# Moving the factor products and gates of a feed-forward layer from second-level into first-level Strassen steps, and another order of the sums at its entry

## What is computed

```python
def layer_tail(x, attn, rw, attn_out_g, w_out, norm_ffn_g, w_gate, w_up, w_down):
    mix = jnp.concatenate([rmsnorm(attn, attn_out_g), rw], axis=-1)
    h = x + mix @ w_out
    u = rmsnorm(h, norm_ffn_g)                      # 1056 x 1024
    return h + (jax.nn.silu(u @ w_gate) * (u @ w_up)) @ w_down     # 2816 hidden columns
```

## Time and profile before

| | |
|---|---|
| median of three runs | 1822.84 us (1821.5 to 1827.82) |
| the profiled execution | 1822.36 us |
| its span, first to last instruction | 1820.6 us |
| mean granted clock of TensorE | 0.983 |
| busy: TensorE, its weight loads | 1724.9 us (95%), 1300.2 us (71%) |
| busy: VectorE, ScalarE, GpSimd | 1046.7 us (57%), 444.9 us (24%), 738.1 us (41%) |
| tail from the end of the out product | from about 950.8 us to the end |
| steps 1 to 51 | 977.4 to 1534.6 us |

### The profile page before, as it was taken

The page is one execution under the profiler, slowest core; times in us unless marked ns, Lnnn a source line. Parts: engine busy times, 40 slices in busy tenths (PEclk is TensorE's granted clock), DMA queues, the critical chain, the costliest instruction groups (busy, mean ns, idle before and its releaser), DMA issues.

```text
span 1820.6 us, 34845 instructions
## 1 busy us (share of the span) xinstructions
PE 1724.9 (95%) x14612; PEld 1300.2 (71%) x14612; DVE 1046.7 (57%) x1703; ACT 444.9 (24%) x987; POOL 738.1 (41%) x551
## 2 busy tenths in 40 slices
PE   6999999999998998999998899999999999999999
PEld 4566666666665656666667777787777887788887
DVE  3767767767767675665257646554554545625422
ACT  3333333334334334665021111111111201000000
POOL 3563664565455440001333434343433431634332
PEclk9999999999999998999998999999999999999999
DMA  9443343334333326110512111111110112333421
GB/s 361 165 140 108 88 134 128 100 102 141 88 119 106 109 65 165 47 47 1 216 50 103 35 35 46 35 47 41 41 38 33 47 35 76 119 95 113 143 92 64
DMA packets 95921, 169.36 MB, mean 93 GB/s; under 512 B 30395, under 2 KB 64011, under 8 KB 91542
## 3 DMA queue, kind: packets, MB, share of 16 engines
q1 hardware_dynamic: 87302, 119.29, 20.8%
q10 hardware_dynamic: 8464, 47.85, 7.5%
HBM read 136.40 MB, written 23.04 MB: 88 GB/s over the span
## 4 chain that ended last, share of the span: by engine, by line
PE 41%; DVE 9%; issue 1%; ACT 0%; DVEq 0%
PE psum L2811 37%; PE psum L2764 4%; DVE hid L3325 2%; DVE hid L3277 1%; DVE hid L3291 1%; DVE hid L3279 1%; DVE hid L3392 0%; DVE mixT L3393 0%; DVE u2c L3339 0%; DVE u2c L3350 0%; DVE u2c L3336 0%; DVE u_sum L3398 0%; PE psum L2799 0%; DVE u2c L3334 0%; DVE u2c L3357 0%
## 5 line engine op out<-in xcount | busy, mean ns | idle before, releaser
L2811 PE MATMUL psum<-mixT,wA 128*128 128x264 f32 x996 | 237.7, 390 | 0.0
L2811 PEld LDWEIGHTS psum<-mixT,wA 128*128 128x128 f32 x996 | 192.2, 193 | 34.0
L535 PE MATMUL psum<-wsl,xt 128*128 128x368 f32 (+2 forms) x716 | 190.2, 441 | 2.8 <-ACT proj L1182 1.7
L2811 PE MATMUL psum<-hid,wA 128*128 128x264 f32 x614 | 150.1, 398 | 26.3 <-DVE u2c L3336 25.7
L2811 PEld LDWEIGHTS psum<-hid,wA 128*128 128x128 f32 x614 | 118.1, 194 | 50.5 <-DVE u2c L3336 29.5
L535 PEld LDWEIGHTS psum<-wsl,xt 128*128 128x128 f32 (+1 forms) x716 | 100.0, 169 | 61.5 <-issue 11.3
L2811 PE MATMUL psum<-u_sum,wA 128*128 128x264 f32 x532 | 130.2, 389 | 5.1 <-ACT con L3000 3.2
L3090 POOL TENSOR_TENSOR wA<-wA 128x512 f32<-128x512 f32 x22 | 29.1, 1324 | 231.4 <-DMA wA<-in_w_up 122.5
L2811 PEld LDWEIGHTS psum<-u_sum,wA 128*128 128x128 f32 x532 | 101.1, 191 | 25.0 <-ACT con L3000 4.4
L2811 PE MATMUL psum<-slot,wA 128*128 128x264 f32 x480 | 111.8, 386 | 3.2 <-DVE slot L3409 3.2
L2811 PEld LDWEIGHTS psum<-slot,wA 128*128 128x128 f32 x480 | 91.1, 190 | 19.1 <-DVE u_sum L3398 3.6
(11 more groups left out here) (427 smaller groups left out, 3514.5 us busy)
## 6 DMA issues: line engine op xcount, KB each, us to landing
wsl<-in_w_in ACTq DMA_DIRECT2D x18, 1472.0 KB, 6.2
wA<-in_w_down SPq DMA_DIRECT2D x30, 704.0 KB, 4.3
slot<-in_w_in ACTq DMA_DIRECT2D x9, 1472.0 KB, 6.8
wA<-in_w_gate SPq DMA_DIRECT2D x44, 256.0 KB, 3.0
wA<-in_w_up SPq DMA_DIRECT2D x44, 256.0 KB, 2.9
mixed<-proj SPq DMA_DIRECT2D x8, 784.0 KB
xt<-in_x_tiles SPq DMA_DIRECT2D x9, 512.0 KB, 6.0
hid<-in_x_cols SPq DMA_DIRECT2D x8, 528.0 KB, 7.1
```

What stands on the lines that cost most here:

```text
L535: return pe.matmul(out, lhsT, rhs, start=start, stop=stop)
L2811: ins = pe.matmul(pb[bank][:, 0:NW], left(k), right(k), start=first and k == 0, stop=k == depth - 1, skip_group_check=not first)
```

## The change

For each quadrant of each unit a new function `home` names one first-level step and a slot in it: `EARLY_` (behind the sum `c11`, ahead of `c12`), `OWN` (between `c12` and `c21`) or `LATE_` (at the end). A quadrant that is complete after a first- or second-level step goes to the next first-level step. Quadrant 11 of a unit that isn't folded stays in its own step. Exceptions stand in `home`: double 0 goes to steps 6 and 8, the two quadrants 12 of double 7 stay at the end of their second-level step 39, and what is complete last (double 10) is done in step 51. `tasks(i, slot)` gives the gate quadrants, of which at most three go to the early slot and the rest to `OWN`, and the up quadrants. VectorE's new `gates` makes factor product j + 1 before gate product j; ScalarE makes `tanh` in the same order, in first-level steps ahead of `p5c` and `u2c`.

```diff
+        if q == 12 and not gate_unit(d, b) and not cut_in_two(d, 3):
+            return done, OWN
+        if q == 11 and not folded:
+            return at_step[1, F, 0] if d == 0 else done, EARLY_
+        if d == N_D - 1 and (folded or b):
+            return N_STEPS - 1, LATE_ if folded else EARLY_
+        if q == 12 and d == LATE_END - 1:
+            return done, LATE_
+        if d == 0:
+            first = not folded and b == 0 or q == 11
+            return (at_step[1, F, 0], EARLY_) if first else (at_step[1, F, 1], EARLY_)
+        if d == 1 and b == 0 and q in (11, 21):
+            return at_step[2, F, 0], EARLY_
+        i = done + 1
+        while STEPS[i][1] != F:
+            i += 1
+        return i, EARLY_
...
+        def gates(found):
+
+            for j, x in enumerate(found):
+                scale(x)
+                if j:
+                    gate(found[j - 1])
+            if found:
+                gate(found[-1])
...
         def first_level(i, d, b):
...
-            scales(early_scaled.get(i, []))
-            gates(i)
+            opened, found = tasks(i, EARLY_)
+            head = [x for x in found if x[0] == 22]
+            ups(head)
+            gates(opened)
+            ups([x for x in found if x not in head])
+            if i == at_step[0, F, 1]:
+                token_sums_of(2, 0, 4)
+                token_sums_of(3, 0, 4)
+            if i == at_step[N_D - 1, F, 1]:
+                down_sums_begun()
             if i == 0:
-                row_means()
+                row_factors()
...
             named(tt(two(place(12, d, b)), bank_pair(W), two(u2c), ALU.add), "c12_ok", n)
-            scales(own_third(i))
-            if i == 0:
-                row_factors()
+            opened, found = tasks(i, OWN)
+            ups(found)
+            gates(opened)
```

```diff
+        def down_sums_begun():
+
+            dve.wait_ge(s["hid_ok"], n_hid(at_step[N_D - 1, F, 0]))
+            c1 = slice(HT, HT + NW)
+            B12, B22 = hid[:, 0:FH - 1, c1], hid[:, FH:2 * FH - 1, c1]
+            named(tt(B12, B22, B12, ALU.subtract), "f3_ok", 1)
...
             if i == 0:
+                row_sums()
                 pe.wait_ge(s["t3_ok"], 1)
-                row_sums()
             pe.wait_ge(s["s3_ok"], u + 1)
             for nh in range(2):
                 pe.wait_ge(s["u2_ok"], 2 * n - 1 + nh)
                 product(X + nh, left(S3), half(B12u, nh), KH, "p7_ps", first=False)
-                if i == 0 and nh == 0:
-                    row_factors()
+            if i == 0:
+                row_factors()
```

More of the change, by code:

```diff
@@ L2586, in bank, with home @@
         return pb[i][:, 0:NW]
-    scaled_in, gated_in = {}, {}
+    EARLY_, OWN, LATE_ = 0, 1, 2
+    homes = {}
+    def home(x):
+        q, d, b = x
+        k = INNER.get(q, 0)
+        folded = k and after(d, b, k)
+        done = at_step[d, S, k] if folded else at_step[d, F, b]
+        if q == 12 and not gate_unit(d, b) and not cut_in_two(d, 3):
[15 more added lines that the diff above has]
+        return i, EARLY_
@@ L2605, in tail @@
-    own_third = lambda i: [x for x in scaled_in.get(i, []) if x == (12, STEPS[i][0], STEPS[i][2]) and STEPS[i][1] == F]
-    late_scaled = {i: [x for x in found if INNER.get(x[0], 0) and after(x[1], x[2], INNER[x[0]])] for i, found in scaled_in.items()}
-    early_scaled = {i: [x for x in found if x not in late_scaled[i] + own_third(i)] for i, found in scaled_in.items()}
+            for q in (22, 21, 11, 12):
+                homes.setdefault(home((q, d, b)), []).append((q, d, b))
+    is_gate = lambda x: gate_unit(*x[1:])
@@ L2609, in gate_of, with tasks @@
+    def tasks(i, slot):
+        early, own = homes.get((i, EARLY_), []), homes.get((i, OWN), [])
+        opened = [x for x in early if is_gate(x)]
+        ups = [x for x in early if not is_gate(x)]
+        if slot == EARLY_:
+            return opened[:3], sorted(ups, key=lambda x: x[0] != 22)
+        if slot == OWN:
+            return opened[3:], own
+        late = homes.get((i, LATE_), [])
+        return [x for x in late if is_gate(x)], [x for x in late if not is_gate(x)]
     def gate_of(x):
@@ L2993, in _ @@
             weighted(k, slice(0, TOK), "u_lo")
+        squares(KD - 2)
         act.wait_ge(s["ps_done"], 2 * KD)
@@ L2997, in _ @@
             weighted(k, slice(HT, TOK), "u_hi1")
+        squares(KD - 1)
         for k in (4, 5):
@@ L3021, in first_level @@
                 copy(two(place(11, d, b)), bank_pair(X)).then_inc(s["p1_ok"], 1)
-            if i == 0:
-                for last in (KD - 2, KD - 1):
-                    squares(last)
-            for x in early_scaled.get(i, []):
-                if gate_unit(*x[1:]):
-                    tanh(x)
+            for x in tasks(i, EARLY_)[0]:
+                tanh(x)
             all_read(i - 1)
+            if any(x[0] == 22 for x in tasks(i, EARLY_)[1]):
+                act.wait_ge(s["hid_ok"], n_hid(i - 1) + 1)
             act.wait_ge(s["p5_ps"], n)
@@ L3046, in second_level @@
             copy(first_in, bank(X)).then_inc(s["m1_ok"], 1)
-            for x in late_scaled.get(i - 1, []):
-                if gate_unit(*x[1:]):
-                    tanh(x)
             if not folds(d, k, 1):
@@ L3065, in _ @@
                 second_level(i, d, n)
-        for x in late_scaled.get(N_STEPS - 1, []):
-            if gate_unit(*x[1:]):
-                tanh(x)
         for n in range(len(DOWN)):
@@ L3360, in second_level @@
                 named(tt(o12, W, v2, ALU.add), "v12_ok", n)
-            last = late_scaled.get(i, [])
-            if i < N_STEPS - 1:
-                scales(last)
-                gates(i)
-            else:
-                scales([x for x in last if gate_unit(*x[1:])])
-                gates(i)
-                scales([x for x in last if not gate_unit(*x[1:])])
+            opened, found = tasks(i, LATE_)
+            gates(opened)
+            ups(found)
         for i, (d, what, n) in enumerate(STEPS):
```

91 lines of the change are left out of this document (34 added, 57 removed).

## The result

The changed kernel takes 1764.07 us as a median (1763.07 to 1764.33) against 1822.99 us (1821.5 to 1827.82): a ratio of 0.967, with a 95% interval of 0.965 to 0.969. That is 58.9 us, where 53 were forecast. The profiled execution took 1763.07 us, its span is 1761.3 us, and the mean granted clock rose from 0.983 to 0.992.

A forecast was written before the change was run, and what follows sets the result against it. TensorE, busy 95%, was taken as the bound, with time won only where it waits, mostly for VectorE, or runs at low clock. Entry 7.0 + steps 43 + down product 3.0 = 53 us off, 1769.8 as median, range 1762 to 1788.

The forecast's parts named there:

- The steps: Steps 1 to 51: waits and half clock, together 45.7 us, go, less 1 and 1.5 for new waits: 43 us gained.
- the wait of step 8: First-level step 8, which also has an up product and two more gates: a new cost of 1 us.
- the other one: Behind step 39, which keeps two up products at its end: u2c late for the next step, 1.5 us.
- t: Time of one VectorE multiplication in first-level steps, taken as 0.8 us; no wait up to 1.06 us in the L3299 steps.
- the formula: First-level steps: 4.5 + 4t + 1.94 = 10.7 in L3299 steps, 6.6 + 2t = 10.7 in steps starting with p11's copy.
- Rival 1: First-level steps: multiplications take 1.66 us there too, u2c comes 2.4 us late in five steps, 20 us, 1790; chance 0.12.
- rival 4: Eleven first-level steps with gates: three tanh delay p5c and u2c; slower from t = 2.9 us, about 1832; chance 0.03.
- The entry: Entry before step 1: earlier squares and sums let row sums start without a wait; 8.0 less 1.0 for clock, 7.0 us.
- rival 2: Entry: row sums and transposes let the clock fall to half, 4 to 5 us more, 1774; chance 0.15.
- The down product: First group of the down product: waits of 0.7 and 3.2 us go, 3.9, less 0.9 half clock: 3.0 us gained.

The follow-up runs named there:

- ups_after_v3: Changed kernel with the two up products at the end of step 39 made in step 40 behind its sums v22 and v21: 1764.41 us.
- best: Changed kernel with step 39's up products in step 40, GpSimd's first wide down-product sum held back, product five started on ten blocks: 1755.62 us.
- gates_plus1: Changed kernel with one more VectorE multiplication, which changes nothing, ahead of each of the 44 factor products: 1765.93 us.
- four_early: Changed kernel with up to four instead of three gates in the early slot, ahead of ScalarE's p5c and u2c: 1765.1 us.
- gates_plus3: Changed kernel with three more VectorE multiplications, which change nothing, ahead of each factor product: 1842.67 us, ratio 1.011 to the kernel before.
- entry_back: Changed kernel with the old order at the entry (squares, their sums, row sums, row factors, row means, token sums): 1772.88 us.
- f3_whole: Changed kernel with the first operand sum of the down product (f3) whole again, behind the last hidden result: 1764.7 us.
- before_again: The kernel before the change, unchanged, profiled a second time: 1821.17 us, down product 287.80 us.
- lone_steps: Changed kernel with six factor and six gate products of doubles 2, 4 and 6 put back into second-level steps between first-level ones: 1765.63 us.
- e3_later: Changed kernel with GpSimd's first 1408-wide sum of the down product held until VectorE has made the last up product: 1760.89 us.
- f3_whole_again: Second profile of the changed kernel with the operand sum f3 whole again: 1764.89 us, down product 287.80 us.

## Why the prediction was right

**The sign, the mechanism and the range were right; the sum was 6 us short.** 53 forecast, 58.9 measured, 1764.07 within 1762 to 1788.

**The steps: 43 forecast, 47.6 measured.** The count of the prediction settles it, with one figure put right: sixteen records start 3.56 us apart, 0.2225 us each and not 0.222, so 2280 of them are 507.3 us and not 506. The steps without a wait in ups_after_v3 and best, 507.40 us, bear that out. Before, the steps took 49.6 us more: 35.0 in waits and other long gaps, 13.0 by half clock, 1.7 in small gaps (rounded). After, 2.0 more: 1.8 in one gap, 0.2 in small ones, no half clock. So the idle time and the half clock went whole, as the sum had it. The 4.4 us between its 43.2 and 47.6 are 2.2 that idle time and clock were short (45.7 of 47.9; the idle time was put 4 us too low and the half clock 2 too high), 1.5 of the small gaps, 1.0 for the wait of step 8 that did not come, less 0.3 for the other one's size. That one came where it was put, as a wait of 1.6 us for 1.5 (step 39 and 40 of after):

```profile
1333.78 3.35 DVE L3293 SCALAR_TENSOR_TENSOR hid<-hid 128x528 f32<-128x528 f32 x2
...
1337.99 1.16 PE L2836 MATMUL psum<-hid,wA 128*128 128x264 f32 x4 [1.63 <-DVE u2c L3372]
```

**The room in the first-level steps.** t = 0.8 us was taken by the row it was nearest to, GpSimd idle in the middle of such a step. Step 13 of after, one of the four that begin with the sum L3299 (here L3327), from its first matmul:

```profile
1075.43 3.72 PE L2836 MATMUL psum<-mixT,wA 128*128 128x264 f32 x16
...
1079.25 0.71 DVE L3327 TENSOR_TENSOR hid<-psum,hid 128x528 f32<-128x528 f32 x1 [3.03 <-PE psum L2836]
...
1082.14 0.71 DVE L3291 TENSOR_TENSOR hid<-hid,proj 128x528 f32<-128x528 f32 x1
...
1082.89 0.64 ACT L3034 ACTIVATE proj<-hid 128x528 f32<-128x528 f32 x1 [0.90 <-DVE hid L3291]
1083.44 0.59 ACT L3027 ACTIVATE p5c<-psum 128x528 f32<-128x528 f32 x1
...
1084.53 0.39 ACT L3027 ACTIVATE u2c<-psum 128x264 f32<-128x264 f32 x1 [0.50 <-PE psum L2836]
1086.11 4.61 PE L2836 MATMUL psum<-mixT,wA 128*128 128x264 f32 x20
```

The third tanh starts at +7.5, u2c at +9.1, which is where it stood before, and not because of the tanh: it waits for its product. S3 starts at +10.7. The multiplications take 0.70 to 0.71 us here, so the 0.8 was generous. Over the run (a line, as in the earlier trace rows):

```profile
L3291 DVE TENSOR_TENSOR hid<-hid,proj x44: 699/708/1766, 1008.5 to 1479.9; 128x528 f32<-128x528 f32 x44
```

The median of the factor product fell from 784 to 708 ns; those in steps that start with the copy of p11 take 0.9 to 1.2 us beside GpSimd's 256-wide sums, and the formula left them up to 2. The maximum, 1.77 us, is in step 45, beside a 512-wide sum. Rival 1 needed 1.66 us in the L3299 steps and fell on this. gates_plus1 and four_early show that the room is real and ends where the formula looked for it, at S3. It is 1.8 us and not 1.4, with the hand-over of 1.57 us: in gates_plus1 three more instructions of 0.70 us, 2.1 us, made the copy 0.23 us late. And gates_plus3 that rival 4's chain (VectorE, third tanh, p5c, u2c, S3) is one that can make the kernel slower than before.

**The entry: 7.0 forecast, 9.05 measured.** The timeline of after, beside the earlier trace rows:

```profile
956.31 2.55 DVE L3219 TENSOR_TENSOR hid<-hid 128x1056 f32<-128x1056 f32 x2
...
961.80 1.99 PE L2824 MATMUL psum<-hid 128*128 128x1 f32 x18
...
967.39 1.21 PE L2830 MATMUL psum<-con,row_ms 128*128 128x128 f32 x9
968.53 1.16 PE L2836 MATMUL psum<-u_sum,wA 128*128 128x264 f32 x4
```

The sums end at 958.86 (forecast 958.8), the row sums start at 961.80 without a wait and take 1.99 us (bounds 1.8 and 3.7), the transposes 1.21 (bounds 0.9 and 1.8), and step 1 starts at 968.53, within 968.2 to 970.9. Of the 2 us that were missed one is the us taken off for rival 2, since the clock stayed at 1.00, and one the choice of 8.0 within 6.6 to 9.3, which had row sums and transposes longer than they are at full clock. The entry_back kernel has the same work behind a wait of 4.6 us (961.4 to 966.0), and there the clock was 0.81 in the mean. Two stretches of it, with the columns of the earlier trace rows, show when it fell:

```profile
961.30:964.40 3.10, 0.09 (x1) 0.00 (x0) 3.00 (x4) 0.39 (x1) 0.00 (x0) 1.00 0.51 202
964.40:974.60 10.20, 8.60 (x32) 7.67 (x33) 3.09 (x7) 0.00 (x0) 1.79 (x1) 0.50 0.00 0
```

That is 1.6 us before the first row sum (966.00): the fall came in the wait, and the row sums didn't start it. Whether they made it longer no run shows.

**The down product: 3.0 forecast, 2.7 measured, and in part by luck.** The term took the 6.07 us of f3 as its price beside GpSimd. That is one of two values (6.0 to 6.1 us in three executions with f3 whole, 3.18 in two), and f3_whole shows the other: without the cut the down product can be as short as with it. Against before_again, 287.80 us, the gain would have been 4.35. The forecast that f3's ten blocks would fit into step 50 held: they took 2.91 us there (2.8 forecast), and no wait of TensorE is in the steps for it. The half clock, put at the mean of 0 and 1.7, cost 1.5: 3.4 us at 0.50 behind a single wait of 2.9 us, which the first wait of 1.2 and the second of 1.8 have become. By TensorE's gaps the 2.7 are 4.1 us less idle time, less 1.5 of half clock, and 0.1 in small gaps. Behind the last matmul nothing changed (3.54 and 3.55 us).

**SBUF's lock.** The Trainium skill, "SBUF — State Buffer", section "SBUF: two separate sides", says that whichever of VectorE and GpSimd starts first keeps the shared ports for its whole instruction and the other blocks. The wide sums of this case agree: 3.18 us against 6.02, decided by 0.1 to 0.3 us, and 0.71 against 3.47 for the last up product, which ends 0.6 us behind GpSimd's sum. The prediction drew from it t up to 1.42 us in the first-level steps and a gain of 45 us; in after the multiplications of those steps take at most 1.23 us beside 256-wide sums (0.73 us alone), 1.77 us once in step 45 beside a 512-wide one, and no wait of TensorE comes from it.

**What stays open.** Why a wait of about 3 us in the same place was followed by 0, 3.4 or 6.8 us of half clock (after 3.4, ups_after_v3 6.8, lone_steps 0, each behind 2.9 us), and in the kernel before a wait of 3.2 us by none in one execution and by 3.4 us in the other; no run separates it, and it moves the time by up to 3.4 us. Nor was it run what the multiplications would cost in the pairs of second-level steps alone.

## What to carry to other kernels

Where one engine feeds another in steps of different length, count for each step what it owes before its deadline; multiplications that nobody waits for belong into the steps with room, and the room is found from the deadline of the consumer (here the copy ahead of S3), not from busy shares. Count a wait of TensorE with the half clock that may follow it: here 13 us lost to the clock went with 35 us of idle time. And where a VectorE sum and a wide GpSimd sum can start within some tenths of a microsecond of each other, its time in one trace is one of two values: order the two (e3_later, 2.5 us for one wait on an idle engine) rather than shorten one.

## What the runs showed of the hardware

- Two wide sums that read SBUF twice, on VectorE and GpSimd, don't share: the first to start takes its own time (3.18 or 3.25 us), the second nearly the sum of both (6.02 or 5.88). A 0.71 us multiplication took 3.47 us behind a sum of 3.59. Beside GpSimd's 256-wide sums in a row a multiplication of VectorE grew from 0.70 to 0.9 to 1.23 us only; beside a 512-wide one it took 1.77 us (after).
- Nine matmuls of one column (18 records, 1.99 us) and nine transposes (1.21 us) between dense products left the granted clock at 1.00 (after).
- Waits of 0.2 to 0.9 us (gates_plus1) and of 1.6 us (step 40) left the clock at 1.00; one of 2.4 us (f3_whole_again) was followed by 3.4 us at 0.50, and waits of 2.9 to 3.3 us by 0, 3.4 or 6.8 us. The kernel before, run twice, shows 0 and 3.4 us behind the same wait of 3.2 us.
- ScalarE starts a tanh 0.04 us after the VectorE instruction that it waits for has ended (1082.85 and 1082.89 in step 13 of after), and the copy behind it 0.55 us after the tanh's start, though the tanh's record is 0.64 us long: summing durations of ScalarE's records overstates its queue.
